# Stick-breaking and cross attention on one core: queries and keys turned by transposing DMAs as f16 halves instead of by TensorE in f32

## The reference, cut to what matters

```python
proj = h @ w_in                      # 1024 -> 3072, the part that both attentions and the LRU share
q = rmsnorm(heads(sb_q), sb_q_g)     # 8 heads x 64
k = rmsnorm(heads(sb_k), sb_k_g)
z = q . k * 64 ** -0.5               # stick-breaking attention, strictly causal
w = sigmoid(z) * exp(sum of log(1 - sigmoid) over the keys between)
xq = rmsnorm(heads(xa_q), xa_q_g)    # 4 heads x 64, softmax over 256 memory tokens
mk = rmsnorm(heads(memory @ w_mem_kv), xa_k_g)
out = x + concat(sb * silu, lru * silu, xa * silu) @ w_out
```

## Time and profile before

| | before |
|---|---|
| median of 3 runs | 1676.84 us (1676.5 to 1677.05) |
| profiled execution, its own time | 1676.09 us |
| span of the profiled execution | 1674.1 us |
| PE (matmuls) busy | 1585.6 us, 95% |
| DVE (VectorE) busy | 1033.0 us, 62% |
| ACT (ScalarE) busy | 828.3 us, 49% |
| POOL (GpSimd) busy | 264.4 us, 16% |
| DMA engines busy | 40% of the span |

### The profile page before, as it was taken

One profiled execution on the slowest core, in us unless ns is written; L12 is line 12 of the kernel. 1 busy time (PEld: TensorE's weight loads), 2 busy tenths in 40 slices (PEclk: granted clock), 3 DMA queues, 4 the chain that ended last, 5 costly groups with the idle time before them and its releaser, 6 DMA issues.

```text
span 1674.1 us, 28733 instructions
## 1 busy us (share of the span) xinstructions
PE 1585.6 (95%) x10566; PEld 805.0 (48%) x10566; DVE 1033.0 (62%) x1916; ACT 828.3 (49%) x1487; POOL 264.4 (16%) x245
## 2 busy tenths in 40 slices
PE   2885999999999999999999999999999999999976
PEld 1443455555545555555455555545555555455542
DVE  4876666556665666566666566656666566666662
ACT  5854554445455544555554445455544455555440
POOL 0111111111111110111111101111111111111100
PEclk9987999999999999999999999999999999999987
DMA  9412434334344343433434434344343343434342
GB/s 377 161 32 69 108 95 113 108 93 113 88 107 106 101 119 84 117 94 95 118 94 113 110 91 119 85 103 113 95 118 95 105 102 99 107 99 109 95 95 64
DMA packets 263966, 180.37 MB, mean 108 GB/s; under 512 B 212928, under 2 KB 229632, under 8 KB 262784
## 3 DMA queue, kind: packets, MB, share of 16 engines
q1 hardware_dynamic: 263648, 179.85, 40.0%
q10 hardware_dynamic: 288, 0.13, 0.0%
HBM read 70.60 MB, written 50.53 MB: 72 GB/s over the span
## 4 chain that ended last, share of the span: by engine, by line
PE 89%; issue 4%; DVE 3%; ACT 2%; DMA 1%; POOL 1%; SPq 0%; POOLq 0%; DVEq 0%; ACTq 0%
PE bank L1334 26%; PE bank L1335 25%; PE bank L1336 25%; PE bank L1355 2%; PE bank L1394 2%; PE bank L1421 2%; PE bank L1412 2%; PE bank L1448 2%; DVE w_pair L902 1%; DMA ident<-ident_flat 1%; PE bank L1478 0%; PE bank L1473 0%; PE bank L1475 0%; PE bank L1474 0%; PE bank L1431 0%
## 5 line engine op out<-in xcount | busy, mean ns | idle before, releaser
L1334 PE MATMUL bank<-w_pair,x_hi 128*128 128x512 f16 x1536 | 586.8, 382 | 9.9 <-DVE w_pair L902 5.0
L1335 PE MATMUL bank<-w_pair,x_hi 128*128 128x512 f16 x1536 | 585.7, 381 | 0.0
L1336 PE MATMUL bank<-w_pair,x_lo 128*128 128x512 f16 x1536 | 585.2, 381 | 0.0
L1334 PEld LDWEIGHTS bank<-w_pair,x_hi 128*128 128x128 f16 x1536 | 151.2, 98 | 184.9 <-issue 14.5
L1336 PEld LDWEIGHTS bank<-w_pair,x_lo 128*128 128x128 f16 x1536 | 151.1, 98 | 183.7 <-issue 4.5
L1335 PEld LDWEIGHTS bank<-w_pair,x_hi 128*128 128x128 f16 x1536 | 151.2, 98 | 168.7 <-issue 3.3
L1025 DVE TENSOR_REDUCE ss<-turned 128x8 f32<-128x512 f32 (+1 forms) x96 | 57.3, 597 | 240.5 <-ACT turned L672 169.1
L1334 PE MATMUL bank<-wo_pair,y_hi 128*128 128x512 f16 x512 | 196.3, 383 | 7.9 <-DMA y_lo<-spare 7.9
L1335 PE MATMUL bank<-wo_pair,y_hi 128*128 128x512 f16 x512 | 196.1, 383 | 0.0
L1336 PE MATMUL bank<-wo_pair,y_lo 128*128 128x512 f16 x512 | 195.9, 383 | 0.0
L526 POOL TENSOR_TENSOR fail_and_take<-fail_and_take,seen 128x512 f32<-128x512 f32 x32 | 40.5, 1264 | 786.8 <-ACT fail_and_take L665 786.8
(11 more groups left out here) (212 smaller groups left out, 2413.1 us busy)
## 6 DMA issues: line engine op xcount, KB each, us to landing
xy<-in_x SPq DMA_DIRECT2D x32, 512.0 KB, 3.3
x_t<-in_x_turned SPq DMA_DIRECT2D x32, 512.0 KB, 4.3
spare<-in_x SPq DMA_DIRECT2D x32, 512.0 KB, 4.2
out<-spare SPq DMA_DIRECT2D x32, 512.0 KB, 2.6
wo_pair<-in_w_in SPq DMA_DIRECT2D x4, 2048.0 KB, 10.2
gate_kept<-gate SPq DMA_DIRECT2D x32, 256.0 KB, 2.0
v_kept<-v_sb SPq DMA_DIRECT2D x32, 256.0 KB, 2.1
fail_and_take<-v_sb SPq DMA_DIRECT2D x64, 128.0 KB, 2.3
```

What stands on the lines that cost most here:

```text
L1334: pe.matmul(dst, hi[:, k, :], pair[:, 0, k, :], start=k == 0, stop=False)
L1335: pe.matmul(dst, hi[:, k, :], pair[:, 1, k, :], start=False, stop=False)
L1336: last = pe.matmul(dst, lo[:, k, :], pair[:, 0, k, :], start=False, stop=k == KD - 1)
```

## The change

Queries and keys leave TensorE's transposes. After the row factors have been multiplied in, ScalarE writes the high f16 halves of `q_raw`, `k_raw`, `xq_raw` (scaled by 2^11, the keys also by the inverse of their gain's power of two), VectorE the low halves, into the space that y's halves use later in the step. SP turns each of the six halves with a transposing DMA straight into `q_t`, `k_t`, `xq_t`, which are f16 now. The gains of both sides are multiplied together: into `k_raw` by a new GpSimd instruction, and into the memory's keys. The scores become three f16 products each. The halo of the keys is copied from SBUF by two ScalarE copies. The high halves of y, of the weights and of `probs` are turned as soon as they are there, without waiting for the low ones. `rs_diag` moves into `spare` (for the first two tiles into `tanh_l`), chunk 7 is split 5 to 3 instead of 2 to 6, and some waits are added for buffers that are now shared.

```diff
-        k_t = sb("k_t", [P, 2, HS // 2, HALF + P])
-        q_t = sb("q_t", [P, HS // 2, P])
-        xq_t = sb("xq_t", [P, HX // 2, P])
+        k_t = sb("k_t", [P, 2, 2, HS // 2, HALF + P], F16)
+        q_t = sb("q_t", [P, 2, HS // 2, P], F16)
+        xq_t = sb("xq_t", [P, 2, HX // 2, P], F16)
...
+        def halves_of_heads(n, part):
+            if isinstance(n, int) and n == 0:
+                qk, xq = first_halves[:, part], first_xq_halves[:, part]
+            else:
+                qk, xq = y_halves[:, part], xq_halves[:, part]
+            return qk[:, 0:GC], qk[:, GC:2 * GC], xq
...
-            return [slice(0, KD // 2), slice(KD // 2, KD)] if c == 6 else [slice(0, 2), slice(2, KD)]
+            return [slice(0, KD // 2), slice(KD // 2, KD)] if c == 6 else [slice(0, 5), slice(5, KD)]
```

In `body` of SP:

```diff
                 if C:
+                    have(sp, s["y_high"], n - 2)
+                    have(sp, out_done[1], n - 3)
+                    turn(y_hi[:, :, :], y_halves[:, 0, :], y_turned)
                     have(sp, s["y_low"], n - 2)
-                    have(sp, out_done[1], n - 3)
-                    turn(y_hi, y_halves[:, 0, :], y_turned)
-                    turn(y_lo, y_halves[:, 1, :], y_turned)
+                    turn(y_lo[:, :, :], y_halves[:, 1, :], y_turned)
...
                 if B:
-                    have(sp, s["w_low"], n - 1)
+                    have(sp, s["w_high"], n - 1)
...
                     turn(turned[:, 0], halves[:, 0, :], w_turned)
+                    have(sp, s["w_low"], n - 1)
                     turn(turned[:, 1], halves[:, 1, :], w_turned)
+                if A:
+                    if isinstance(n, int) and n == 0:
+                        sp.wait_ge(w_sum, CH)
+                    have_dma(sp, kept["q"], n - 1)
+                    have(sp, s["xa_scores"], n - 1)
+                    for part, signal in ((0, s["qk_high"]), (1, s["qk_low"])):
+                        have(sp, signal, n)
+                        q_half, k_half, xq_half = halves_of_heads(n, part)
+                        turn(q_t[:, part], q_half, qk_turned)
+                        turn(k_t[:, p, part, :, HALF:], k_half, qk_turned)
+                        turn(xq_t[:, part], xq_half, qk_turned)
                 if A:
                     have_dma(sp, kept["gate"], n - 1)
                     keep("gate", gate_kept, gate[:, p, 0:GC], n, [s["gate_sb"]])
                 if B:
                     have(sp, s["heads"], n - 1)
+                    have(sp, s["p_high"], n - 1)
+                    turn(turned[:, 0], halves[:, 0, :], p_turned)
                     have(sp, s["p_low"], n - 1)
-                    turn(turned[:, 0], halves[:, 0, :], p_turned)
                     turn(turned[:, 1], halves[:, 1, :], p_turned)
```

In `body` of POOL, ahead of `rs`:

```diff
+                    have(pool, s["k_read"], n)
+                    pool.tensor_tensor(k_raw[:, :, :], k_raw[:, :, :], k_gain[:, :].unsqueeze(1).to_broadcast([P, HS, HD]),
+                                       ALU.mult).then_inc(s["k_gained"], 1)
```

In `body` of ACT, at the start of stage B, and behind the activations of `lru_read`:

```diff
-                    act.activation(k_t[:, p, :, 0:HALF], keys[:, :, HALF:P], ACT.Copy, scale=gk[:, :])
-                    act.activation(k_t[:, q, :, HALF:], keys, ACT.Copy, scale=gk[:, :]).then_inc(s["k_evac"], 1)
+                    have(act, qk_turned, n - 1, 96)
+                    for part in range(2):
+                        last = act.activation(k_t[:, p, part, :, 0:HALF], k_t[:, q, part, :, P:], ACT.Copy)
+                    last.then_inc(s["k_halo"], 1)
...
+                    have(act, s["normed"], n)
+                    have_turned(act, y_turned, n - 2)
+                    have(act, qk_turned, n - 1, 96)
+                    for raw, half in zip((q_raw, k_raw, xq_raw), halves_of_heads(n, 0)):
+                        scale = QTOP if raw is not k_raw else gain_inv[:, 0:1]
+                        last = act.activation(half, raw[:, :, :].rearrange("p h d -> p (h d)"), ACT.Copy, scale=scale)
+                    last.then_inc(s["qk_high"], 1)
```

ACT, ahead of the activation that gives `y_high`:

```diff
+                    if A:
+                        have(act, qk_turned, n, 96)
```

In `body` of DVE the turned operands are no longer read from the bank:

```diff
-                    dve.tensor_scalar(q_t[:, :, :], TURN[0][:, :].rearrange("p (c t) -> p c t", t=P), gq[:, :], None,
-                                      ALU.mult).then_inc(s["q_evac"], 1)
-                    dve.tensor_scalar(xq_t[:, :, :], SMALL[:, 0:2 * P].rearrange("p (c t) -> p c t", t=P), gxq[:, :], None,
-                                      ALU.mult)
```

DVE, behind the instruction that gives `gate_l`:

```diff
+                    have(dve, s["qk_high"], n)
+                    for raw, high, low in zip((q_raw, k_raw, xq_raw), halves_of_heads(n, 0), halves_of_heads(n, 1)):
+                        scale = QTOP if raw is not k_raw else gain_inv[:, 0:1]
+                        last = dve.scalar_tensor_tensor(low, raw[:, :, :].rearrange("p h d -> p (h d)"), scale, high,
+                                                        ALU.mult, ALU.subtract)
+                    last.then_inc(s["qk_low"], 1)
```

In `body` of PE:

```diff
-                    for c in range(4):
-                        turn(q_raw[:, 2 * c:2 * c + 2, :].rearrange("p h d -> p (h d)"), TURN[0][:, c * P:(c + 1) * P])
-                    for c in range(4):
-                        turn(k_raw[:, 2 * c:2 * c + 2, :].rearrange("p h d -> p (h d)"), TURN[1][:, c * P:(c + 1) * P])
-                    for c in range(2):
-                        turn(xq_raw[:, 2 * c:2 * c + 2, :].rearrange("p h d -> p (h d)"), SMALL[:, c * P:(c + 1) * P])
...
-                        for top in (0, HALF):
-                            for odd in range(2):
-                                r = slice(odd * HD, (odd + 1) * HD)
-                                last = pe.matmul(SCORE[odd][top:top + HALF, c * HW:(c + 1) * HW],
-                                                 q_t[r, c, top:top + HALF], k_t[r, q, c, top:top + HW],
-                                                 start=True, stop=True)
+                        for a, b in ((0, 0), (0, 1), (1, 0)):
+                            for top in (0, HALF):
+                                for odd in range(2):
+                                    r = slice(odd * HD, (odd + 1) * HD)
+                                    last = pe.matmul(SCORE[odd][top:top + HALF, c * HW:(c + 1) * HW],
+                                                     q_t[r, a, c, top:top + HALF], k_t[r, q, b, c, top:top + HW],
+                                                     start=a + b == 0, stop=a == 1)
...
+                    for c in range(HX // 2):
+                        for a, b in ((0, 0), (0, 1), (1, 0)):
+                            for odd in range(2):
+                                r = slice(odd * HD, (odd + 1) * HD)
+                                last = pe.matmul(SCORE[odd][:, c * NM:(c + 1) * NM], xq_t[r, a, c, :], mk_t[r, b, c, :],
+                                                 start=a + b == 0, stop=a == 1)
```

More of the change, by code:

```diff
@@ L160, in hybrid_layer @@
         rate = few(LH)
+        k_gain = sb("k_gain", [P, HD])
+        gain_top = few(2)
+        gain_exp = few(2)
+        gain_inv = few(2)
+        near_scale = few(2)
+        past_scale = few(2)
+        mk_gain = few(1)
         tiny = sb("tiny", [P, 6, LH])
@@ L304, in have_dma, with diagonal_of @@
             have(eng, signal, tile, 16)
+        def halves_of_heads(n, part):
[4 more added lines that the diff above has]
+            return qk[:, 0:GC], qk[:, GC:2 * GC], xq
+        def diagonal_of(tile):
+            return tanh_l[:, 0, :] if isinstance(tile, int) and tile < 2 else rs_diag
         def have_turned(eng, signal, tile):
@@ L415, in body @@
                     have_dma(sp, kept["k"], n - 2)
-                    keep("q", q_kept, q_t[:, :, :], n - 1, [s["q_evac"]])
-                    keep("k", k_kept, k_t[:, q, :, HALF:], n - 1, [s["k_evac"]])
+                    have(sp, qk_turned, n - 1, 96)
+                    keep("q", q_kept, q_t[:, :, :, :], n - 1, [])
+                    keep("k", k_kept, k_t[:, q, :, :, HALF:], n - 1, [])
                     have_dma(sp, kept["carry"], n - 2)
@@ L465, in row @@
             def row(i, w, before, n_steps):
-                for dst, src in ((q_t[:, :, :], q_kept[i]), (gate[:, 0, 0:GC], gate_kept[i]),
+                for dst, src in ((q_t[:, :, :, :], q_kept[i]), (gate[:, 0, 0:GC], gate_kept[i]),
                                  (carry[:, 0, :], carry_kept[i]), (x_res, out_t[i])):
@@ L1408, in body @@
                     have(pe, s["sig"], n - 1)
-                    have(pe, s["xqc_evac"], n - 1)
-                    for h in range(HX):
-                        r = slice((h % 2) * HD, (h % 2 + 1) * HD)
-                        last = pe.matmul(SCORE[h % 2][:, (h // 2) * NM:(h // 2 + 1) * NM], xq_t[r, h // 2, :],
-                                         mk_t[r, h // 2, :], start=True, stop=True)
+                    for c in range(HX // 2):
[4 more added lines that the diff above has]
+                                                 start=a + b == 0, stop=a == 1)
```

(7 more changed lines are left out.)

139 lines of the change are left out of this document (81 added, 58 removed).

## The result

The changed kernel takes **1743.45 us** (median of 4 runs, 1741.62 to 1744.49) against 1676.78 for the kernel before on the same chip: ratio 1.0396, 95% interval 1.0378 to 1.0414. It is 4% slower where 3% faster was forecast, and lies outside the forecast range.

What follows compares the result with a forecast made beforehand. PE was taken to bound the kernel, busy throughout each 48.20 us step. Saving 1.45 us a step, 43.5 over 30 steps, plus 2.3 in the head and 2.7 in the tail, from 1676.09 gave 1628 us; range 1617 to 1652.

Steps and rivals of the forecast that it cites:

- SP term: SP's queue: issuing six new turns takes 3.7 us, bounds 3.3 and 7.8; nothing charged for the probabilities.
- rival 3: SP's queue: 1.3 us for each turn whatever its size, PE stops 1.5 us a step, kernel 1673; chance 0.08.
- Turns gone: PE, each step: the ten transposes of q, k and xq go, saving 1.09 us.
- scores: PE, each step: three f16 products instead of four passes, 0.82 us instead of 1.03, saving 0.21.
- cross scores: PE, each step: 6 pairs of f16 products plus 0.20, from 1.06 us, saving 0.21.
- Rivals 2, 4 and 5: PE's small products: no gain, 1671, chance 0.08; f16 takes turns, 1704, 0.05; only row halves share, 1647, 0.02.
- ACT and DVE: Three high-half copies cost ACT 1.4 us, DVE's low halves are free; 0.06 us a step charged for `rs_diag`.
- DVE's scan: DVE beside POOL's new multiply: the scan loses 0.5 to 0.7 us, hidden by 0.68 us of slack.
- rival 1: ACT's chain is late: PE waits 0.3 to 0.8 us a step for `rs_diag` or `probs`, 1635 to 1650; chance 0.12.
- Turning the high half early is what saves this: SP, each step: with `probs`' high half turned early, the low half lands at 834.3, PE asks at 835.0.
- Head and tail: Start and end of the kernel: head -2.3 us, bounds -6 and +4; tail -2.7, bounds 0 and -5.

Runs made afterwards that it cites:

- five: The changed kernel with the turn of xq's low half done for the first tile only, five turns a step; 1666.05 us.
- seven: The changed kernel with xq's low half turned a second time into unused space, seven turns a step; 1803.08 us.
- filled: The changed kernel with eight f16 products of 512 columns a step, never read, ahead of PE's wait for the probabilities; 1706.7 us.
- paired_diag: As `paired`, but DVE makes `rs_diag` ahead of the recurrence's scans instead of behind them; 1629.06 us.
- paired: The changed kernel with q and xq halves side by side, turned by one DMA of 768 columns from the second tile on: four turns for six; 1636.36 us.
- paired_low: As `paired`, but the turn of the probabilities' high half waits for the low half too, as before the change; 1662.76 us.
- early: The kernel before with only the early turns of the high halves of y, `take` and probabilities, and chunk 7 split five to three; 1672.45 us.
- dummies: The kernel before with six transposing DMAs of 256 columns of constants a step in SP's queue, for nobody; 1719.74 us.

## Why the prediction was wrong

- **The step that failed is the SP term**: "I take issuing as proportional to the pieces: 0.7, 0.7, 0.45, twice, 3.7 us". Measured: 1.19, 1.26 and 1.25, twice, 7.7 us with the gaps. The comparison was with a plain DMA, while the price of a transposing one, the nearer in kind, stood beside it as 1.3 a turn and was used for the bounds alone. The prediction's upper bound, 7.8, was the value, and it had said what it would do: rival 3, "PE stops 1.5 us in each step". The stop is 2.21. Counted from the step's first `lx_raw` transpose, PE asks for the probabilities after 40.8 us, as forecast (835.0 - 794.22 and 918.70 - 877.93); they were to land after 40.1 (834.3 - 794.22), "0.7 us in hand, nothing charged", and PE could start after 43.0 (920.91 - 877.93).
- **The chance of rival 3 was therefore too small.** "nothing excludes a fixed price" was written there, and the one row of a transposing DMA, 1.3 us at 1024 columns, fits a fixed price (7.8 us for the six) as well as one by columns (3.3, the lower bound). 0.08 isn't what such an open choice is worth. `five`, the changed kernel and `seven` show the fixed price directly.
- **And rival 3 was under-priced.** It ended at 1673 because it took the lost time to be a wait of 1.5 us alone; 0.5 of the missing 0.7 us lie in the gaps around the gate's DMA (915.47 to 916.36, where it had 0.4). With the stop at 2.21 us the steps would be 46.85 + 2.21 = 49.06, which is the fourth step's 49.10 and the 49.11 of `filled`. The clock adds 1.23 to 1.28 us a step, in sum 37 us (1743.45 - 1706.7). No case of the prediction had it. The trace before had no idle stretch in a steady step from which to learn its size; only its first steps hint at it, with a granted clock of 0.84 from 105.90 to 166.77 us, where PE is busy for 42.65 of 60.87.
- **Terms that held.** Turns gone, scores 0.80 (forecast 0.82), cross scores 0.76 (0.85): PE's own work without any wait is 46.59 us a step (`paired_diag`), and 48.20 - 46.59 = 1.61 saved against 1.09 + 0.42 = 1.51 forecast. Rivals 2, 4 and 5, which had the scores at 1.55, 2.76 and 1.47 us, are out by the 0.80.
- **ACT and DVE** came nearly as forecast: the three copies hold ACT for 1.55 us (906.14 to 907.69) where 1.4 was taken. `rs_diag` is ready at 913.13, and it costs 0.26 us a step (46.85 - 46.59, what making it earlier brought in `paired_diag`) where 0.06 was charged: a mild form of rival 1. DVE's scan loses 3.02 - 2.35 = 0.67 us under POOL's multiply, as forecast, and nobody waits for it. A scan takes 1524 ns in the mean where it took 1215. The Trainium skill (SBUF — State Buffer, "Who interferes with whom") has the rule that a DVE instruction with two inputs in SBUF contends with a GpSimd instruction that reads SBUF. The trace agrees: the multiply runs from 891.05 to 892.32 and the scans begin at 891.51, so they overlap by 0.81 us, of which 0.67 are lost.
- **"Turning the high half early is what saves this"** was right about the mechanism: it is worth 26 us with four turns (`paired` against `paired_low`). Six turns were too many for it all the same.
- **Head and tail**: forecast -2.3 and -2.7. The tail came out at -1.9, of which `early` alone has 1.7. The head came out at +5.6, of which 4.9 lie in step 2 (167.49 to 221.41, 53.92 us for 49.06): against `paired`, where that step is 49.16, PE is idle for 2.1 us more and busy for 2.65 more, at a clock of 0.91 for 0.95. In `paired` the third `lx_raw` transposes come at 215.79, where it was 215.82: the 2.3 us that were forecast didn't come even without the stop.

The parts as measured, on the execution of the earlier trace rows: 1676.1 + 5.6 + 64.0 - 1.9 = 1743.8, for 1743.44 of the profiled execution.

## What to carry to other kernels

Price a queue by the number of its instructions of a kind, taking the price from a row of that same kind, and where no row shows whether the size matters, carry both prices through the sum; four turns for six, with the same bytes, were worth 107 us here. When a new wait of PE appears, ask what the clock does behind it: the stop may cost half as much again. And before moving transfers into a queue, look where in its order they go: the place behind the one that is asked for was worth 96 us, nearly as much as the merging. The two were not tried together.

## What was not expected of the hardware

- A transposing DMA from SP costs 1.2 to 1.3 us to issue (medians) at 256, 512, 768 and 1024 columns alike, and 1.84 at 2048, where the times spread (1337 to 2077 ns); the small ones lie close to their median but for a few near 2000 or 2500. One kind stands apart: the second turn of `take`, of 1024 columns, takes 2.3 to 3.5 us in each steady step of the changed kernel, where the first is issued early. What holds it up is open.
- PE idle for 0.6, 0.8 and 1.2 us a step (`paired_low`, `five`, `dummies`) left the granted clock at 1.00; 2.1 us lowered it in three steps of four, 3.45 in every one. Why some steps escape at 2.1 is open.
- The idle time shown ahead of a product understates what a stop costs when full-size products precede it, by 0.15 to 0.17 us here, since their shown ends lie that far beyond the start of the next one. With losses counted from start to start the steps close: 46.85 + 0.98 = 47.83 (`five`, 47.81), + 0.75 = 47.60 (`paired_low`, 47.62), + 1.73 + 0.52 = 49.10 (`filled`, 49.11).
